# Residual kept in the experts' sum banks, and five or six more buffers for weights

## The chip, the cores and the metric

One core of a Trainium2 chip runs the whole program. The metric is the time of the program on the device in microseconds (us), the median of several executions. The core has a matrix engine (TensorE, PE in the profile), VectorE (DVE), ScalarE (ACT), GpSimd (POOL) and SyncE (SP), which here only issues the DMA transfers. On-chip memory is SBUF (128 partitions) and, for the sums of TensorE, PSUM with eight banks of 512 float32 a partition.

## The reference

A decoder of two layers over 256 tokens of width 1024, all in float32. Layer 0 has a Mamba-2 mixer, layer 1 a sliding-window attention mixer; both also attend to 256 memory tokens. Each layer ends in a mixture of 32 gated experts, of which each token uses two of one group. Cut to what matters:

```python
for layer in range(2):
    h = h + mixer(h)                      # ssd_memory_mixer / swa_memory_mixer
    xt = rms_norm(h)
    gates = route(xt)                     # top-1 group, top-2 experts in it
    out = 0
    for e in range(32):
        he = silu(xt @ w_gate[e]) * (xt @ w_up[e])       # 1024 -> 512
        out = out + gates[:, e:e + 1] * (he @ w_down[e]) # 512 -> 1024
    h = h + out
return rms_norm(h, final_norm_w)
```

One expert's three matrices are 6 MiB, all experts of both layers 384 MiB. Every one is read once.

## The kernel before

**Stages.** `mixer_a`, the experts of layer 0 (`moe(c, 0)`), `mixer_b`, the experts of layer 1, `final_norm`. Each is a block of five instruction streams, one per engine, with semaphores between them; a block starts when all engines have left the one before.

**Weight slots.** Every weight is loaded in pieces of 1 MiB (a "job", `GRAN` = 2048 float32 a partition) into a slot. There are 11 `own` slots, 6 in `late` (in the mixers `late` is working memory) and `extra`: 18. `place_jobs` hands the slots out in turn, oldest first; `free` is the list. SP issues the jobs strictly in order (`load_job`, L255), each after a wait until the job that had the slot before is used (`before`, `released`, in the mixers `tile_used` and `late_free`). In the mixer's block SP issues the mixer's own tiles and then the first `FIRST_JOBS` = 18 jobs of the experts, all that fits; the others are issued in the experts' block.

**Experts.** A layer's 32 experts are eight quads of four. The first four quads in the order of load are worked off as two "wide" units each, of two experts with up to 64 tokens each; the other four as one "narrow" unit each, of four experts with up to 32 tokens. So 12 units, eight of 12 jobs and four of 24. A quad's place is found on the chip: VectorE sorts the quads by their fullest expert (`order`, L1365 to L1381, 13 steps, then `over`), SP and VectorE read the result into registers (`quads`, seven loads). SP does so before job 24, since the jobs before it belong to quad 0, always first. A unit on TensorE: gate and up in two halves (`gate_up`, L1498), gather of the next unit's tokens (L1473, scaled by VectorE in `gathered`, L1343), transposes, down in two halves (`down`, L1507), gates' transposes, and `scatter` (L1490), four matmuls (eight records of the profile) that add to four banks `sums` = banks 0 to 3, started afresh in unit 0. In layer 0 units 9 and 10 are preceded by `side`: keys and values of the memory for layer 1, from `memT1`, into `mkT1` and `mv1`.

**Residual.** The residual h lies in SBUF (8 KiB a partition). The mixer adds its output to it (`Router.dve`, L533); the normalised rows for the experts are written to `xs`. After the experts, `finish_h` (L436) adds the four banks to h, at the head of `mixer_b` and of `final_norm`. After the router TensorE does four matmuls of the identity with constants, whose result nobody uses (`Router.pe`, L517, eight records).

**Overflow.** Experts with more tokens than a unit holds are done in `over_rounds` at the end of the block. It needs the register `most`, which each engine loads there. With these inputs the branch isn't taken.

**Working buffers.** `xbcT`, `xnT`, `qT`, `acc` and small ones of mixer A, `xnT`, `qtok`, `qmT` of mixer B, and the experts' `pick`, `gated`, `xg`, `silu`, `hid`, `turned`, `gates_T`, `y` and `rank` are allocated stage by stage beside the slots.

Of the kernel before, what the change touches and what calls it, by code (L numbers as in the profile page):

```python
# [28 lines left out]
P = 128  # L29
# [22 lines left out]
OWN, LATE = 11, 6  # L52
SLOTS = OWN + LATE + 1
# [54 lines left out]
def place_jobs():  # L108
# [14 lines left out]
    free = free[:-8] + LATE_A + free[-8:]  # L123
    for layer in range(2):
        for job in expert_jobs(layer):
            slot = free.pop(0)
            put(job, slot)
            free.append(slot)
        if layer == 0:
# [6 lines left out]
            free = LATE_B[:2] + own[:-6] + LATE_B[2:] + own[-6:]  # L136
# [10 lines left out]
OVER_SLOTS = [slot for slot in range(SLOTS) if slot not in KEPT]  # L147
# [25 lines left out]
class Core:  # L173


    def __init__(self, nc, ins, out, ctx):
        self.nc, self.ins, self.out, self.ctx = nc, ins, out, ctx
        self.small = self.sb("small", SMALL)
        self.h = self.sb("h", NT * D)
        self.xs = self.sb("xs", NT * D)  # L180
# [13 lines left out]
        self.own = self.sb("own", OWN * GRAN)  # L194
        self.late = self.sb("late", LATE * GRAN)
        self.extra = self.sb("extra", GRAN)
# [5 lines left out]

    def carve_late(self, *sizes):
        assert sum(sizes) <= LATE * GRAN
        return [self.late[:, sum(sizes[:i]):sum(sizes[:i + 1])] for i in range(len(sizes))]
# [22 lines left out]
    def slot(self, job):  # L228
        n = JOB_AT[job][0]
        if n == OWN + LATE:  # L230
            return self.extra[:, :]
        return self.own[:, n * GRAN:(n + 1) * GRAN] if n < OWN else self.late[:, (n - OWN) * GRAN:(n - OWN + 1) * GRAN]
# [66 lines left out]
class Units:  # L299
# [4 lines left out]
    def __init__(self, core, order, freed, holds=None, first=0):  # L304
# [7 lines left out]
        free, user, self.of, self.before = [*range(first, NBANK), *range(first)], {}, {}, {}  # L312
# [133 lines left out]
class Router:  # L446
# [4 lines left out]
    SEMS = "h_new n2_act n2_dve x2T_act x2T_dve rw_ready rt_dve rt_act counted"  # L451
# [46 lines left out]
    def pe(self, pe, key):  # L498
# [123 lines left out]
def mixer_a(c):  # L622
# [12 lines left out]
    with ctx:  # L635
        sb = lambda name, n: c.sb("a_" + name, n, ctx)
        xbcT = sb("xbcT", 12 * SEQ)
# [3 lines left out]
        xnT = sb("xnT", KD * SEQ)  # L641
        mem = memnT
        qT = sb("qT", 1024)
        mT = qT
        acc = sb("acc", 3 * SEQ)
# [3 lines left out]
        cbm2 = sb("cbm", 2 * P)  # L649
# [10 lines left out]
        dtb = [sb(f"dt{i}", 2 * SSD_HEADS) for i in range(6)]  # L660
        dtx, t_, s_, s2, dt, adt = dtb
        ea, eac, toend, acum = sb("ea", 24), sb("eac", 24), sb("toend", 24), sb("acum", 48)
        smc = sb("smc", 64)
        gss = sb("gss", 8)
# [64 lines left out]
        late_free = [U.at["yT", 7]] * 4 + [U.at["mk", 3], U.at["pv", 3], U.at["yo", 3]]  # L729
# [3 lines left out]
        def _(sp):  # L733
# [39 lines left out]
            for job in expert_jobs(0)[:FIRST_JOBS]:  # L773
# [3 lines left out]
                else:  # L777
# [417 lines left out]
class Experts:  # L1195
# [13 lines left out]
    def allocate(self, ctx):  # L1209
        c, layer = self.c, self.layer  # L1210
        sb = lambda name, n: c.sb(f"e{layer}_{name}", n, ctx)
        self.pick = sb("pick", NT * P)
        self.gated = sb("gated", NT * P)
        self.xg = sb("xg", KD * P)
        self.silu = sb("silu", DE)
        self.hid = sb("hid", DE)
        self.turned = sb("turned", DE)
        self.gates_T = sb("gates_T", SEQ)
        self.y = [sb(f"y{i}", 512) for i in range(2)]
        self.rank = sb("rank", 7 * QUADS * QUADS)  # L1220
        self.sums, (self.b_gate, self.b_up, self.b_gather, self.b_turn) = c.banks[0:4], c.banks[4:8]
# [855 lines left out]
```

## Time and profile before

| what | value |
|---|---|
| runs, median (lowest to highest) | 1386.57 us (1385.32 to 1391.3), 3 runs |
| profiled execution, its own time | 1383.7 us |
| its span, first to last instruction | 1381.9 us |
| mean granted TensorE clock | 0.956 |
| PE busy | 1227.8 us, 89% |
| DVE, ACT, POOL busy | 281.3, 203.9, 32.7 us |
| HBM read | 460.91 MB |
| mean over the span | 334 GB/s |

The page cuts the span into 40 slices of 34.5 us; one line gives the GB/s that the 16 DMA engines moved in each. PE's busy time counts overlapping matmuls once, and a busy PE is not PE at its peak. A timeline row gives the start, the duration, the engine and line, the operation, how many alike are merged (xN) and, in brackets, the engine's idle time before it with what ended it. Rows on SPq are issues of transfers; their duration is that of issuing, not of moving data.

### The profile page before, as it was taken

What the parts mean: (1) busy time and instruction counts of PE and PEld (TensorE: products, weight loads), DVE (VectorE), ACT (ScalarE), POOL (GpSimd) and SP (SyncE); (2) the same over time, 40 slices, a digit from 0 to 9 for tenths busy, and PEclk for the clock granted to TensorE, in tenths of its full rate; (3) what the DMA queues carried; (4) which work ended last, traced back from release to release, by engine and by line L of the source; (5) the groups of instructions that cost most, each with busy time, mean ns of one, the idle gap of its engine ahead of it and who ended that gap; (6) DMA issues with size and microseconds to landing.
All of it is one profiled execution on the core that took longest, in us unless ns stands there. A gap on an engine that the chain in (4) does not pass through costs nothing. (4 is left out here: it accounts for less than half of the span.)

```text
span 1381.9 us, 15072 instructions
## 1 busy us (share of the span) xinstructions
PE 1227.8 (89%) x6036; PEld 608.3 (44%) x6036; DVE 281.3 (20%) x683; ACT 203.9 (15%) x488; POOL 32.7 (2%) x42
## 2 busy tenths in 40 slices
PE   6999999999999998877778998999999999657685
PEld 5875764544444443432323566454444444222221
DVE  3842551221111111010102164031111111000101
ACT  2233231300000000000002255120000000000001
POOL 0001200000000000000000011000000000000000
PEclk9999999999999999989899999999999999887897
DMA  9731178479999999999999612559999999999994
GB/s 347 294 122 54 52 286 340 183 304 421 420 422 421 421 422 414 423 416 421 421 421 355 231 61 92 212 196 422 420 422 420 421 421 421 421 421 422 421 421 180
DMA packets 81241, 463.03 MB, mean 335 GB/s; under 512 B 7392, under 2 KB 9488, under 8 KB 32016
## 3 DMA queue, kind: packets, MB, share of 16 engines
q1 hardware_dynamic: 81168, 462.02, 82.3%
q8 instruction: 51, 0.84, 0.2%
q14 instruction: 22, 0.18, 0.0%
HBM read 460.91 MB, written 1.07 MB: 334 GB/s over the span
## 5 line engine op out<-in xcount | busy, mean ns | idle before, releaser
L1498 PE MATMUL bank<-own,e_xg 128*64 128x512 f32 (+1 forms) x1272 | 267.4, 635 | 36.2 <-DMA own<-in_w_gate 10.1
L1498 PE MATMUL bank<-late,e_xg 128*32 128x512 f32 (+1 forms) x648 | 162.9, 648 | 16.2 <-DMA own<-in_w_up 7.7
L1498 PEld LDWEIGHTS bank<-own,e_xg 128*64 128x64 f32 (+1 forms) x1272 | 78.3, 130 | 199.0 <-issue 198.9
L1507 PE MATMUL bank<-own,e_turned 128*64 128x512 f32 (+1 forms) x576 | 131.0, 685 | 32.0 <-DMA own<-in_w_down 19.7
L1390 DVE TENSOR_TENSOR e_hid<-e_silu,bank 128x512 f32<-128x512 f32 x24 | 25.6, 1067 | 502.6 <-ACT e_silu L1441 502.6
L1507 PE MATMUL bank<-late,e_turned 128*32 128x512 f32 (+1 forms) x408 | 94.9, 671 | 25.2 <-DMA own<-in_w_down 11.3
L1473 PEld LDWEIGHTS bank<-e_pick,xs 128*128 128x128 f32 x768 | 89.6, 192 | 19.6 <-issue 19.6
L1473 PE MATMUL bank<-e_pick,xs 128*128 128x128 f32 x768 | 95.5, 278 | 0.0
L1441 ACT ACTIVATE e_silu<-bank 128x512 f32<-128x512 f32 x24 | 14.3, 597 | 539.5 <-PE bank L1498 539.5
L1498 PEld LDWEIGHTS bank<-late,e_xg 128*32 128x32 f32 (+1 forms) x648 | 45.6, 131 | 96.7 <-issue 96.6
L1490 PE MATMUL bank<-e_y,e_gates_T 128*128 128x512 f32 x192 | 86.5, 593 | 1.4 <-ACT e_gates_T L1449 1.4
L1507 PEld LDWEIGHTS bank<-own,e_turned 128*64 128x64 f32 (+1 forms) x576 | 36.7, 137 | 103.0 <-issue 94.1
L401 PE MATMUL bank<-a_xnT,own 128*128 128x256 f32 x320 | 70.1, 380 | 0.0
L1395 DVE COPY e_y<-bank 128x512 f32<-128x512 f32 x24 | 16.6, 691 | 254.3 <-PE bank L1507 254.3
L401 PEld LDWEIGHTS bank<-a_xnT,own 128*128 128x128 f32 x320 | 60.4, 190 | 8.4 <-issue 0.4
L1498 PE MATMUL bank<-extra,e_xg 128*64 128x512 f32 (+1 forms) x128 | 59.7, 610 | 0.0
L1507 PEld LDWEIGHTS bank<-late,e_turned 128*32 128x32 f32 (+1 forms) x408 | 25.8, 134 | 73.1 <-issue 66.2
L1490 PEld LDWEIGHTS bank<-e_y,e_gates_T 128*128 128x128 f32 x192 | 34.6, 190 | 36.3 <-issue 34.4
L1447 ACT ACTIVATE e_y<-bank 128x512 f32<-128x512 f32 x24 | 14.3, 597 | 241.6 <-PE bank L1507 241.6
L1516 PE MATMUL bank<-small 128*128 128x512 f32 x88 | 41.9, 622 | 2.6 <-PEq L1624 1.3
L1343 DVE TENSOR_TENSOR e_xg<-bank,small 128x512 f32<-128x512 f32 x48 | 33.2, 692 | 48.2 <-PE bank L1473 48.2
L401 PE MATMUL bank<-own,a_xnT 128*128 128x512 f32 x96 | 42.1, 593 | 0.0
(357 smaller groups left out, 1124.1 us busy)
## 6 DMA issues: line engine op xcount, KB each, us to landing
own<-in_w_gate SPq DMA_DIRECT2D x81, 1024.0 KB, 13.1
own<-in_w_up SPq DMA_DIRECT2D x78, 1024.0 KB, 12.6
own<-in_w_down SPq DMA_DIRECT2D x72, 1024.0 KB, 13.4
late<-in_w_down SPq DMA_DIRECT2D x51, 1024.0 KB, 13.4
late<-in_w_gate SPq DMA_DIRECT2D x42, 1024.0 KB, 13.6
late<-in_w_up SPq DMA_DIRECT2D x39, 1024.0 KB, 12.5
own<-in_a_in_w SPq DMA_DIRECT2D x17, 1024.0 KB, 14.3
extra<-in_w_up SPq DMA_DIRECT2D x11, 1024.0 KB, 14.4
```

The costliest lines, as they stand in the source:

```text
L401: ins = pe.matmul(out, lhsT(k), rhs(k), start=(k == 0), stop=(k == n - 1))
L1343: dve.tensor_tensor(cut(self.xg[:, 512 * half:512 * half + 512], k=4), cut(bank, k=4), spread_last(c.f(f"ffn_norm{layer}", 4 * half, 4 * h ...
L1390: dve.tensor_tensor(self.hid[:, :].rearrange("q (h j p) -> q h p j", h=2, j=2), by_half(self.silu), by_half(self.b_up), ALU.mult).then_inc ...
L1395: dve.tensor_copy(self.y[1][:, :], self.b_down[1][:, :]).then_inc(s["y_ready"], 1)
L1441: act.activation(self.silu[:, :], self.b_gate[:, :], ACT.Silu).then_inc(s["silu_done"], 1)
L1447: act.activation(self.y[0][:, :], self.b_down[0][:, :], ACT.Copy).then_inc(s["y_ready"], 1)
L1473: ins = pe.matmul(bank[:, k * P:(k + 1) * P], xs[:, t, 4 * half + k, :], cut(self.pick, t=NT)[:, t, :], start=(t == 0), stop=(t == NT - 1))
L1490: ins = pe.matmul(self.sums[2 * t + out][:, :], self.gates_T[:, t * P:(t + 1) * P], self.y[out][:, :], start=first, stop=last, skip_group_ ...
L1498: ins = pe.matmul(bank[q * T:(q + 1) * T, :], self.xg[:, at:at + T], cut(tile(q), k=4)[:, k, :], start=(half == 0 and k == 0), stop=(half ...
L1507: ins = pe.matmul(self.b_down[out][q * T:(q + 1) * T, :], self.turned[:, at:at + T], cut(tile(q), j=2)[:, j, 512 * out:512 * out + 512], s ...
L1516: pe.matmul(self.b_turn[:, :], c.f("ident"), c.small[:, 0:512], start=True, stop=True)
```

## The change

1. `dynamic_dma_scratch_size=512` is given to the program (default before), and with the SBUF that this and the rest frees there are 12 own slots and up to six others: EXTRA as before, XNT (`xnT`), TAIL (the first 8 KiB of one common working buffer `work`), RES (`h`), MKV (`mkT1` and `mv1` together), MEMT (`memT1`). `place_jobs` puts MKV first and TAIL, XNT, RES last in layer 0 and leaves MKV out from unit 9 on; in layer 1 MEMT is first, MKV in the middle and TAIL, XNT, RES last. The mixers load the first 23 and 24 jobs.
2. After the router TensorE multiplies the identity with h into the four sum banks, in place of the four matmuls with constants. The experts' scatter adds to that. The stages after copy the banks (two by VectorE, two by ScalarE) or read them directly in the last norm. The banks are 0, 3, 4, 7 in layer 0 and 0, 5, 6, 7 in layer 1.
3. `order` goes ahead of the two `gathered` of the first unit, since its scratch now shares a buffer with `silu`; `y` shares `silu` and `hid`.
4. The load of `most` goes from the end of the block to the place after `quads` (SP, DVE) and after unit 0 (ACT, PE). The table for the square root is loaded in the last unit. The vector of the final norm is loaded after the last weights instead of at the start of the block.

```diff
-OWN, LATE = 11, 6
-SLOTS = OWN + LATE + 1
+OWN, LATE = 12, 6
+SLOTS = OWN + LATE + 6
+EXTRA, XNT, TAIL, RES, MKV, MEMT = range(OWN + LATE, SLOTS)
+SUMS = [[0, 3, 4, 7], [0, 5, 6, 7]]
+WORK = GRAN + 3328
...
-    free = free[:-8] + LATE_A + free[-8:]
+    free = [MKV] + free[:-8] + LATE_A + free[-8:] + [TAIL, XNT, RES]
     for layer in range(2):
         for job in expert_jobs(layer):
             slot = free.pop(0)
+            if slot == MKV and layer == 0 and (job[0] == "mem" or job[2] >= SIDE[0]):
+                slot = free.pop(0)
             put(job, slot)
             free.append(slot)
...
-            free = LATE_B[:2] + own[:-6] + LATE_B[2:] + own[-6:]
+            free = [MEMT] + LATE_B[:2] + own[:-6] + [LATE_B[2], MKV] + LATE_B[3:] + own[-6:] + [TAIL, XNT, RES]
...
-FIRST_JOBS = SLOTS
+FIRST_JOBS = [SLOTS - 1, SLOTS]
...
-def finish_h(c, dve, q, signal):
-
-    hq = c.h[:, 512 * q:512 * q + 512]
-    dve.tensor_tensor(hq, hq, c.banks[q][:, :], ALU.add).then_inc(signal, 1)
+def copy_h(c, layer, q):
+
+
+    return c.h[:, 512 * q:512 * q + 512], c.banks[SUMS[layer][q]][:, :]
...
-            for _ in range(4):
-                pe.matmul(out[:, :], c.f("ident"), c.small[:, 0:512], start=True, stop=True)
+            pe.wait_ge(s["h_new"], 4)
+            for q in range(4):
+                ins = pe.matmul(c.banks[SUMS[self.layer][q]][:, :], c.f("ident"), c.h[:, 512 * q:512 * q + 512], start=True, stop=True)
+            ins.then_inc(s["h_kept"], 1)
...
-        late_free = [U.at["yT", 7]] * 4 + [U.at["mk", 3], U.at["pv", 3], U.at["yo", 3]]
+        late_free = [U.at["yT", 7]] * 4 + [U.at["mk", 3], U.at["pv", 3], U.at["yo", 3], U.at["router", 1], U.at["out", 3]]
...
-            for job in expert_jobs(0)[:FIRST_JOBS]:
+            for job in expert_jobs(0)[:FIRST_JOBS[0]]:
                 prev, slot = before(job), JOB_AT[job][0]
                 if prev:
                     sp.wait_ge(*tile_used(prev[1]))
-                else:
+                elif slot == RES:
+                    sp.wait_ge(s["h_kept"], 1)
+                    sp.wait_ge(s["n2_act"], 6)
+                elif slot != MKV:
                     sp.wait_ge(c.units_done, late_free[slot - OWN] + 1)
...
+        self.y, self.rank = [self.silu, self.hid], self.silu
+        self.sums = [c.banks[i] for i in SUMS[layer]]
...
-                if layer == 1:
-                    final_w = c.ins["final_norm_w"].rearrange("(o n) -> o n", o=1)
-                    sp.dma_start(c.memT1[:, 0:D], final_w.broadcast_to([P, D])).then_inc(c.final_w, 16)
                 for n, job in enumerate(jobs):
-                    if n < FIRST_JOBS:
+                    if n < FIRST_JOBS[layer]:
                         continue
                     if job == ("expert", layer, 2, "gate", 0, 0):
-                        quad = self.quads(sp)
+                        quad, most = self.quads(sp), self.beyond(sp)
...
                 pick(0)
+                order()
                 for half in range(2):
                     dve.wait_ge(s["gathered"], half + 1)
                     gathered(half, s["xg_ready"], (self.b_gather, self.b_turn)[half])
-                order()
-                quad = self.quads(dve)
+                quad, most = self.quads(dve), self.beyond(dve)
...
-                    ins = scatter(u == 0, last)
+                    ins = scatter()
...
                 for u in range(NU):
                     unit(u)
+                    if u == 0:
+                        most = self.beyond(pe)
...
+            for q in (2, 3):
+                act.activation(*copy_h(c, 0, q), ACT.Copy).then_inc(s["h_act"], 1)
...
-            for q in (0, 2, 1, 3):
-                finish_h(c, dve, q, s["h_whole"])
+            for q in (0, 1):
+                dve.tensor_copy(*copy_h(c, 0, q)).then_inc(s["h_dve"], 1)
...
+                for half in range(2):
+                    act.activation(waste[:, 2 * t + half, :], copy_h(c, 1, 2 * t + half)[1], ACT.Square, scale=1.0 / 32,
+                                   accum_out=ss[:, 2 * t + half:2 * t + half + 1]).then_inc(s["act"], 1)
...
-                hv = cut(c.h, t=NT)[:, t, :]
-                dve.scalar_tensor_tensor(out=hv, in0=hv, scalar=r[t], in1=w, op0=ALU.mult, op1=ALU.mult).then_inc(s["done"], 1)
+                for half in range(2):
+                    to, bank = copy_h(c, 1, 2 * t + half)
+                    dve.scalar_tensor_tensor(out=to, in0=bank, scalar=r[t], in1=w[:, 512 * half:512 * half + 512], op0=ALU.mult,
+                                             op1=ALU.mult).then_inc(s["done"], 1)
...
-    nc = bacc.Bacc("TRN2", target_bir_lowering=False, num_devices=1)
+    nc = bacc.Bacc("TRN2", target_bir_lowering=False, num_devices=1, dynamic_dma_scratch_size=512)
```

## Rows read from the trace of the kernel before

**Rows 1.** GB/s moved in each of the page's 40 slices.

```profile
GB/s 347 294 122 54 52 286 340 183 304 421 420 422 421 421 422 414 423 416 421 421 421 355 231 61 92 212 196 422 420 422 420 421 421 421 421 421 422 421 421 180
```

**Rows 2.** Busy time by stretch, a narrow unit; last columns clock, DMA, GB/s.

```profile
1260.00:1280.00 20.00, 12.74 (x64) 3.16 (x64) 0.00 (x0) 0.00 (x0) 0.00 (x0) 0.66 1.01 421
```

**Rows 3.** Timeline of ScalarE, SiLU of units 1 and 8.

```profile
324.42 0.60 ACT L1441 ACTIVATE e_silu<-bank 128x512 f32<-128x512 f32 x1 [18.60 <-PE bank L1498]
...
530.88 0.60 ACT L1441 ACTIVATE e_silu<-bank 128x512 f32<-128x512 f32 x1 [18.61 <-PE bank L1498]
```

**Rows 4.** Waits of TensorE, 285 to 525 us: sum, times, longest.

```profile
PE bank L1507 <- ACT e_turned L1444: 3.8, 8, 0.5
```

**Rows 5.** Waits of TensorE, 525 to 760 us, the longest.

```profile
PE bank L1507 <- DMA own<-in_w_down: 16.8, 5, 5.8
```

**Rows 6.** Waits of TensorE, 745 to 913 us, the longest of nine.

```profile
PE bank L356 <- ACT late L1781: 3.4, 3, 1.4
```

**Rows 7.** Busy time by stretch, at the first release of layer 0.

```profile
282.00:284.00 2.00, 2.00 (x13) 0.59 (x10) 1.69 (x10) 0.00 (x0) 0.00 (x0) 1.00 0.00 0
...
286.00:288.00 2.00, 2.00 (x12) 0.72 (x10) 0.00 (x0) 0.00 (x0) 0.00 (x0) 1.00 0.85 328
```

**Rows 8.** Timeline of SP's queue, layer 0: transfers issued.

```profile
265.80 1.06 SPq L255 DMA_DIRECT2D own<-in_w_gate  x2
284.62 0.80 SPq L255 DMA_DIRECT2D own<-in_w_up  x2
...
291.49 0.81 SPq L255 DMA_DIRECT2D late<-in_w_down  x2
296.61 0.90 SPq L255 DMA_DIRECT2D late<-in_w_gate  x2
...
314.11 0.81 SPq L255 DMA_DIRECT2D own<-in_w_up  x2
```

**Rows 9.** Timeline around the start of the experts of layer 1.

```profile
903.72 0.80 SPq L255 DMA_DIRECT2D own<-in_w_gate  x2
...
906.89 3.68 PE L517 MATMUL bank<-small 128*128 128x512 f32 x8
...
924.03 0.33 SPq L255 DMA_DIRECT2D late<-in_w_up  x1
```

**Rows 10.** Timeline of the routing and first unit, layer 0.

```profile
268.96 3.68 PE L517 MATMUL bank<-small 128*128 128x512 f32 x8
...
275.47 0.43 DVE L1332 TENSOR_TENSOR e_pick<-small,pos 128x256 f32<-128x256 f32 x1 [0.33 <-PEq L635]
...
279.25 0.69 DVE L1343 TENSOR_TENSOR e_xg<-bank,small 128x512 f32<-128x512 f32 x1 [3.35 <-PE bank L1473]
...
281.64 0.18 DVE L1365 TENSOR_REDUCE e_rank<-counts 128x8 f32<-128x32 f32 x1
...
284.59 0.29 DVE L1381 SCALAR_TENSOR_TENSOR over<-pos,e_rank 128x32 f32<-128x32 f32 x2
...
289.19 0.43 DVE L1338 TENSOR_TENSOR e_gated<-e_pick,gates 128x256 f32<-128x256 f32 x1 [4.31 <-issue]
```

**Rows 11.** Timeline from the last scatter of layer 0 into the mixer.

```profile
739.14 3.67 PE L1490 MATMUL bank<-e_y,e_gates_T 128*128 128x512 f32 x8 [0.70 <-ACT e_gates_T L1449]
...
744.04 2.48 DVE L436 TENSOR_TENSOR h<-h,bank 128x512 f32<-128x512 f32 x4 [5.22 <-PEq L1287]
...
745.38 3.40 PE L340 MATMUL bank<-small,h 128*128 128x128 f32 x16 [2.57 <-DVE h L436]
```

**Rows 12.** Timeline of the last norm.

```profile
1372.45 2.48 DVE L436 TENSOR_TENSOR h<-h,bank 128x512 f32<-128x512 f32 x4 [5.59 <-PEq L1287]
...
1373.82 1.04 ACT L1977 ACTIVATE xs<-h 128x1024 f32<-128x1024 f32 x1
...
1377.50 1.28 DVE L1993 SCALAR_TENSOR_TENSOR h<-h,norm_r,memT 128x1024 f32<-128x1024 f32 x1
```

**Rows 13.** DMA queues: kind, packets, MB, share of 16 engines.

```profile
q1 hardware_dynamic: 81168, 462.02, 82.3%
```

More of the change, by code:

```diff
@@ L201, in sb, with carve, carve_work @@
         return (ctx or self.ctx).enter_context(self.nc.sbuf_tensor(name, [P, n], F32))
+    def carve(self, whole, *sizes):
+        return [whole[:, sum(sizes[:i]):sum(sizes[:i + 1])] for i in range(len(sizes))]
     def carve_late(self, *sizes):
         assert sum(sizes) <= LATE * GRAN
-        return [self.late[:, sum(sizes[:i]):sum(sizes[:i + 1])] for i in range(len(sizes))]
+        return self.carve(self.late, *sizes)
+    def carve_work(self, *sizes):
+        assert sum(sizes) <= WORK
+        return self.carve(self.work, *sizes)
     def sem(self, name):
@@ L229, in slot @@
         n = JOB_AT[job][0]
-        if n == OWN + LATE:
-            return self.extra[:, :]
+        if n >= OWN + LATE:
+            return {EXTRA: self.extra, XNT: self.xnT, TAIL: self.work[:, 0:GRAN], RES: self.h, MKV: self.mkv1, MEMT: self.memT1}[n][:, :]
         return self.own[:, n * GRAN:(n + 1) * GRAN] if n < OWN else self.late[:, (n - OWN) * GRAN:(n - OWN + 1) * GRAN]
@@ L299, with __init__ @@
 class Units:
-    def __init__(self, core, order, freed, holds=None, first=0):
+    def __init__(self, core, order, freed, holds=None, first=()):
         self.core, self.freed = core, freed
@@ L311, in __init__ @@
         held = [key for keys in holds.values() for key in keys]
-        free, user, self.of, self.before = [*range(first, NBANK), *range(first)], {}, {}, {}
+        free, user, self.of, self.before = [*first, *[b for b in range(NBANK) if b not in first]], {}, {}, {}
         for key in order:
@@ L659, in mixer_a @@
         yT = xbcT[:, 0:12 * SEQ]
[L660 to L664, printed above, removed]
+        dtx, t_, s_, s2, ea = c.carve(c.memT1, 48, 48, 48, 48, 24)
+        eac = c.over[:, 0:24]
         def channels(j):
@@ L1207, in __init__, with allocate @@
         self.side = SIDE if layer == 0 else []
-    def allocate(self, ctx):
+    def allocate(self):
         c, layer = self.c, self.layer
[L1211 to L1221, printed above, removed]
+        _, self.pick, self.gated, self.xg, self.silu, self.hid, self.turned, self.gates_T = c.carve_work(
+            GRAN, NT * P, NT * P, KD * P, DE, DE, DE, SEQ)
+        self.y, self.rank = [self.silu, self.hid], self.silu
+        self.sums = [c.banks[i] for i in SUMS[layer]]
+        self.b_gate, self.b_up, self.b_gather, self.b_turn = (c.banks[i] for i in range(NBANK) if i not in SUMS[layer])
         self.b_down = [self.b_gate, self.b_up]
@@ L1485, in turn_gates, with scatter @@
                     ins.then_inc(signal, 1)
-                def scatter(first, last):
+                def scatter():
                     for t in range(NT):
@@ L1667, in freed @@
                     "out": (s["h_new"], i + 1)}[kind]
-        U = Units(c, order, freed, holds, first=4)
+        U = Units(c, order, freed, holds, first=[b for b in range(NBANK) if b not in SUMS[0]])
         R = Router(c, U, s, 1, xnT, qmT[:, 0:512])
@@ L1696, in _ @@
                     c.load_mixer_half(sp, n, half)
-            for job in expert_jobs(1)[:FIRST_JOBS]:
+            for job in expert_jobs(1)[:FIRST_JOBS[1]]:
                 prev, slot = before(job), JOB_AT[job][0]
@@ L1700, in _ @@
                     sp.wait_ge(*tile_used(prev[1]))
-                elif late_free[slot - OWN] is not None:
+                elif slot == RES:
+                    sp.wait_ge(s["h_kept"], 1)
+                    sp.wait_ge(s["n2_act"], 6)
+                elif slot == MKV:
+                    sp.wait_ge(c.units_done, U.at["pv", 3] + 1)
+                elif slot != MEMT and late_free[slot - OWN] is not None:
                     sp.wait_ge(c.units_done, late_free[slot - OWN] + 1)
@@ L1956, in final_norm @@
 def final_norm(c):
-    s = c.sems("final", "h_whole act dve done")
+    s = c.sems("final", "act dve done")
     stored = [c.sem(f"stored{t}") for t in range(NT)]
-    w = c.memT1[:, 0:D]
-    ss, r = ([v[:, t:t + 1] for t in range(NT)] for v in (c.norm_ss, c.norm_r))
+    w, waste = c.memT1[:, 0:D], cut(c.work[:, 0:4 * 512], q=4)
+    ss, r = c.norm_ss, ([c.norm_r[:, t:t + 1] for t in range(NT)])
     with c.nc.Block() as block:
```

99 lines of the change are left out of this document (48 added, 51 removed).

## The prediction

> **What bounds the kernel now.** I read the GB/s line of the page first [rows 1]. It has two flat stretches: from the tenth slice to the twenty-first and from the twenty-eighth to the thirty-ninth, the two expert stages, it stands at 414 to 423. In the two mixers it falls to 52 and 61. So the whole kernel moves its bytes at one rate, and loses time where it moves none. The expert weights are 192 transfers of 1 MiB in each layer, plus four for the memory keys in the first; at 421 GB/s one takes 1.0486/0.421 = 2.49 us.
>
> Next, whether that stream or TensorE sets the end of an expert stage. The SiLU of unit 1 stands at 324.42 and that of unit 8 at 530.88 [rows 3]: 206.46/7 = 29.49 us for a unit of 12 transfers, which need 12 x 2.49 = 29.9 us. In these eight "wide" units TensorE never waits for a transfer; its only wait is 3.8 us on a copy [rows 4]. So TensorE is barely faster than the stream there and eats its reserve by 0.4 us a unit. The four narrow units have 24 transfers (59.8 us) for about the same TensorE work. There it waits for weights (16.8 us for one kind alone) [rows 5] and is busy 12.74 of 20 us with the stream at 421 [rows 2]. The end of both expert stages is therefore the last weight's landing: the moment from which the stream ran without a gap, plus what was still to load. In the second mixer, between the stages, its longest sum of waits is 3.4 us, on a copy, and none is on a DMA [rows 6]. So filling more slots before the unbroken stream begins takes 2.49 us a slot off the end, as long as the slots are filled in time that is idle today.
>
> The idle time: in the first layer the stream stands still at 282 to 284 and is at 328 GB/s in 286 to 288, after the first release at 284.62 [rows 7, 8]. That is a lag of about 1.5 us from issue to data, so data flow without a break from 286.1. In the second the last prefill is issued at 903.72 (four MB at most behind it), and the next load only at 924.03 [rows 9], data from 925.5.
>
> **The change, part by part.** *More slots.* The first layer starts with 23 filled instead of 18, the second with 24 instead of 18. The DMAs are the same in number and bytes; they only move ahead. The two kinds:
> - MKV, the twelfth own slot, and in the second layer MEMT are free long before; the GB/s line shows the room (183 in the eighth slice, 196 in the twenty-seventh) [rows 1].
> - TAIL, XNT and RES come free only in the routing. First layer: TAIL with the last own pair, at 265.8 [rows 8]; XNT when the router's matmuls end, before 268.96; RES when the four identity matmuls have read h. They stand where the four warming matmuls stand today, 268.96 to 272.64 (eight records) [rows 10], so about 272.7; SP's queue holds only this load until then. Data: from 267.3, four transfers until 277.3, RES until 279.8. Margin to 286.1: 6 us. Second layer: two own and TAIL at 903.72, data 905.2 to 912.7; XNT to 915.2; RES, free at 906.89 + 3.68 = 910.6 [rows 9], to 917.7. Margin to 925.5: 8 us.
>
> Gain 5 x 2.49 = 12.5 us and 6 x 2.49 = 14.9 us.
>
> *What SP must do at a worse moment.* Before job 24 SP reads the order of the quads, now eight register loads instead of seven. Before, that was the seventh load of the stage and hidden behind the backlog: SP finished an issue at 291.49 + 0.81 = 292.30, the next came at 296.61 [rows 8]; VectorE has the same 4.31 us gap, for the same seven loads, ahead of its instruction at 289.19 [rows 10]. So 0.62 us each, 4.9 us for eight. In the first layer job 23 still waits for the first release; then come the loads, then job 24. Issues at 284.62 and 284.62 + 0.4 + 4.9 = 289.9; data of job 23 run 286.1 to 288.6, those of job 24 begin at 291.4. The stream is idle 2.8 us: cost 2.8 us (bounds: nothing, if the loads overlap the wait, and 4.9 us). Behind SP only the loads are queued; after 291.4 eleven jobs can be queued by 305 (until 318.8), the next is issued at 314.11 [rows 8], so no second gap. In the second layer 24 slots are filled, so the loads come before the first wait. Order ends 5.5 us before the first release (279.1 and 284.62, worked out below), the loads take 4.9. Cost nothing.
>
> *The order of quads moves ahead of the scaling of the gathered rows.* It takes 284.59 + 0.29 - 281.64 = 3.2 us. The pick ends at 275.90, so order runs to 279.1; the first half of the gather lets VectorE go at 279.25 [rows 10]. Hidden with 0.1 us to spare: taken as nothing, at most 0.5 us a layer; 3.2 us a layer if that gather were not there to cover it.
>
> *Residual in the sum banks.* The identity matmuls are 512 columns wide like those which they replace; the mask that follows is the later event or equal. Nothing; bound 1 us a layer, if TensorE starts them late. The scatters accumulate in any case: unchanged. The shared buffers (y in those of silu and hid) add no wait, since TensorE does the scatter before the next unit's gate and up, which come before the next silu.
>
> *Stage ends.* The scatter ends at 739.14 + 3.67 = 742.8, the next stage's first instruction is at 744.04: 1.2 us, of which 0.62 is the register load of the overflow count, now done after unit 0. Then four adds take 2.48 us on VectorE, and TensorE starts before the fourth, at 745.38 [rows 11]. Now two copies on VectorE beside two on ScalarE: TensorE starts after one of each, 0.69 us like VectorE's other 512-column reads of a bank [rows 10]. Saved: 0.62 + (745.38 - 744.04 - 0.69) = 1.3 us; bounds 0.6 and 2. The load on TensorE's queue after unit 0, 0.6 us, falls in the wide units, where TensorE has slack to the stage's end.
>
> *Last norm.* From 1372.45 to 1378.78 [rows 12] it is 6.3 us: two adds (1.3), square (1.04 + 0.1), scale, root and reciprocal (0.8), product 1.28, then the second half's scalars and product. After: squares of two banks (2 x 0.7 from ScalarE's 0.60 for 512 columns [rows 3] and its accumulator read), scalars 0.7, two products of 0.69, scalars 0.6, two products: 1.4 + 0.7 + 1.4 + 0.6 + 1.4 = 5.5. Saved 0.8, and 0.6 for the register load: 1.4 us; bounds 0 and 2.5. The final gain vector (0.5 MB, 1.25 us of the stream) is loaded behind the last weights, in place of the stage's start; TensorE works on those weights for 3.6 us and scatters for 3.7 before the vector is wanted. Nothing.
>
> *Sum.* 12.5 - 2.8 + 14.9 + 1.3 + 1.4 = 27.3 us. The profiled execution took 1383.7 us, 2.9 us under the median 1386.6 (0.2%), so it gives 1356.4, and beside the median **1359.3 us**, 2.0% faster.
>
> **Two rules weighed.** The stream runs at about 421 GB/s in the flat slices [rows 1]. The Trainium skill, "DMA: Bandwidth & Descriptors", section Specifications, gives about 358 GB/s as the HBM limit of a core; by it a slot would be worth 2.93 us and the eleven slots 32.2 us instead of 27.4, an estimate from that page; the trace disagrees with it and decides. The second speaks to the scratch: the queue of kind hardware_dynamic moved 462.02 of the 463.03 MB, and no queue of a software kind is listed [rows 13]. The Trainium skill's "SBUF — State Buffer", section on the size of SBUF, says that the scratch is the ring for software-generated descriptors; by it the shrunken scratch costs nothing here.
>
> **Rivals.**
> 1. *The forecast*, 70%: 1353 to 1366 (from the bounds: gap at SP 0 to 4.9, stage ends and norm up to 2 less or 2 more, clock of the last units, some 2 us).
> 2. *The wide units become the bound.* If a unit rises over 29.9 us, the stream starves and gives the lead back. At 30.9 us, seven units in two layers: 14 us lost, 1373. For it: the margin is only 0.4 us. Against: no instruction is added within a unit. 7%.
> 3. *The three late slots come too late*, since SP waits for them in order: only two and three slots count, 5 x 2.49 + 2.7 - 2.8 = 12.4 us, about 1374. Against: margins of 6 and 8 us. 7%. A further 7% for smaller losses together, 1364 to 1376.
> 4. *No change*: the lead is gained, but the stream breaks later and ends with today's last transfer. The next release comes just when the backlog of the first refill ends (286.1 + 12 x 2.49 = 316.0; the issue at 314.11 [rows 8] gives data from 315.6). But the backlog grows by 0.4 us a unit. About 1384, with the stage ends alone; 5%.
> 5. *Slower: fewer transfers in flight.* Should the hardware queue use the scratch, transfers would come one after another, each with the lag of 1.5 us: 352 transfers, +528 us, some 1890. It decides from 0.08 us a transfer (27.3/352). Against it: the queue kinds [rows 13]. 4%.
>
> **How the numbers follow.** Likeliest 1359.3. The range 1352 to 1373 takes in case 1 with the bounds and most of 2 and the smaller losses; left out are parts of 2, 3, 4 and 5, about 18%. Case 1's own range is 1353 to 1366. Half a per cent is 7 us, about what a measurement can tell. Faster 0.91 (cases 1 to 3), same 0.05, slower 0.04.
>
> **What would show it.** DMA idle before the first release should shrink to about 5 us in the first expert stage, followed by one load, a dip of some 3 us, and then 421; the second starts with no dip. The unit period stays 29.5 us. The first narrow waits for weights come later, the second mixer starts 9 to 10 us earlier and the last sum about 26 us earlier. Wrong, if the unit period is over 29.9, if the stream has holes in the wide units, if RES's load is issued after the first release, or if the rate itself falls below 415.

## The result and the profile after

The changed kernel takes 1351.76 us (median of 4 runs, 1350.94 to 1353.17) against 1385.94 us for the one before: ratio 0.9746, 95% interval 0.9726 to 0.9766, 34.2 us or 2.5% less. The forecast was 1359.3 with 1352 to 1373. The direction and most of the mechanism were right; the time is 7.5 us below the forecast and 0.2 us below the range. Measured once more later, the same kernel took 1353.79 us, inside the range, so that edge alone says little. What the forecast lacked is a mechanism, shown below. The profiled execution took 1350.94 us (span 1349.2) against 1383.7: 32.8 us less, where the sum had 27.3.

The bytes moved in each of the page's slices, in GB/s, after; it answers to [rows 1].

```profile
GB/s 359 328 125 25 47 252 424 188 307 427 427 427 426 427 427 424 427 424 427 427 427 367 319 63 125 187 219 417 426 426 424 425 425 426 426 427 427 426 427 180
```

From the tenth slice to the twenty-first and from the twenty-ninth to the thirty-ninth the stream moves 424 to 427 GB/s, not 414 to 423. No part of the change was costed as touching that rate. At 427, one transfer of 1 MiB takes 1.0486/0.427 = 2.456 us instead of 2.49.

SP's queue in layer 0, in the timeline of the kernel after (start us, duration, place, operation, tiles); it answers to [rows 8].

```profile
266.72 0.43 SPq L270 DMA_DIRECT2D work<-in_w_down  x1
269.24 0.33 SPq L270 DMA_DIRECT2D xnT<-in_w_down  x1
272.75 0.33 SPq L270 DMA_DIRECT2D h<-in_w_down  x1
284.70 0.33 SPq L270 DMA_DIRECT2D mkv<-in_w_down  x1
289.94 0.90 SPq L270 DMA_DIRECT2D own<-in_w_gate  x2
```

The same stretch by windows, after (the columns of [rows 2]; the last is GB/s); it answers to [rows 7].

```profile
280.00:284.00 4.00, 4.00 (x24) 1.95 (x24) 0.71 (x2) 0.00 (x0) 0.00 (x0) 1.00 0.02 4
286.00:288.00 2.00, 2.00 (x12) 0.65 (x10) 0.85 (x2) 0.00 (x0) 0.00 (x0) 1.00 0.77 303
288.00:290.00 2.00, 2.00 (x12) 0.65 (x10) 0.00 (x0) 0.00 (x0) 0.00 (x0) 1.00 0.44 184
290.00:292.00 2.00, 2.00 (x12) 0.72 (x10) 0.00 (x0) 0.00 (x0) 0.00 (x0) 1.00 0.44 86
292.00:294.00 2.00, 2.00 (x12) 0.64 (x10) 0.00 (x0) 0.00 (x0) 0.00 (x0) 1.00 0.98 406
```

This part reads like the forecast. TAIL (work), XNT and RES (h) are issued at 266.72, 269.24 and 272.75, against 265.8, "before 268.96" and about 272.7 predicted. The stream is empty before the first release at 284.70, one load follows, then a dip, and the next issue is at 289.94 (predicted 289.9).

SiLU of units 1 and 8 in ScalarE's timeline, after; it answers to [rows 3].

```profile
324.50 0.60 ACT L1453 ACTIVATE work<-bank 128x512 f32<-128x512 f32 x1 [18.60 <-PE bank L1514]
...
530.96 0.60 ACT L1453 ACTIVATE work<-bank 128x512 f32<-128x512 f32 x1 [18.61 <-PE bank L1514]
```

206.46/7 = 29.49 us a unit, to the hundredth what it was. The wide units did not become slower; but at 427 GB/s their twelve transfers now need 12 x 2.456 = 29.47 us, so the stream and TensorE are level there.

From the last unit of layer 0 into the second mixer, timeline of the kernel after; it answers to [rows 11].

```profile
704.98 1.28 ACT L1459 ACT_TABLE_LOAD   x1
...
723.73 3.67 PE L1506 MATMUL bank<-work 128*128 128x512 f32 x8 [0.70 <-ACT work L1463]
...
727.94 1.28 ACT L1736 ACT_TABLE_LOAD   x1 [4.35 <-PEq L1298]
727.97 1.29 DVE L1913 COPY h<-bank 128x512 f32<-128x512 f32 x2 [4.55 <-PEq L1298]
729.23 1.09 ACT L1736 ACTIVATE h<-bank 128x512 f32<-128x512 f32 x2
...
729.97 1.94 PE L355 MATMUL bank<-small,h 128*128 128x128 f32 x16 [2.57 <-ACT h L1736]
...
735.76 1.28 ACT L1758 ACT_TABLE_LOAD   x1
```

The scatter starts at 723.73 against 739.14: 15.4 us earlier, where the forecast said 9 to 10. VectorE's first instruction of the next block stands 727.97 - 727.40 = 0.57 us after its end, against 744.04 - 742.81 = 1.23 before. These 0.66 us fit the 0.62 of the register load that was moved out of the way; no run moves it alone. But TensorE starts 729.97 - 727.97 = 2.00 us after that instruction, against 745.38 - 744.04 = 1.34 in [rows 11]: ScalarE's first copy waits for a table load of 1.28 us (it puts another set of ScalarE's function tables in place), and TensorE waits for that copy. The two cancel.

The end, timeline of the kernel after; it answers to [rows 12] and, for the scatter, stands against 1367.19 before.

```profile
1334.03 3.67 PE L1506 MATMUL bank<-work 128*128 128x512 f32 x8 [0.70 <-ACT work L1463]
...
1338.38 1.28 ACT L1997 ACT_TABLE_LOAD   x1 [4.49 <-ACTq L1298]
1339.67 0.60 ACT L1997 ACTIVATE work<-bank 128x512 f32<-128x512 f32 x1
...
1340.96 1.28 ACT L2000 ACT_TABLE_LOAD   x1
...
1344.68 1.41 DVE L2014 SCALAR_TENSOR_TENSOR h<-bank,norm_r,memT 128x512 f32<-128x512 f32 x2
```

The last scatter starts 33.2 us earlier (forecast: about 26). From its start to the end of the last product it is 12.06 us, where it was 1377.50 + 1.28 - 1367.19 = 11.59: the last norm lost 0.5 us instead of saving 1.4. Its first function waits for one table load and its root for a second. Before, one load stood at the head of that block, beside the first two of VectorE's adds of [rows 12], which took about as long:

```profile
1372.41 1.28 ACT L1974 ACT_TABLE_LOAD   x1 [5.37 <-PEq L1287]
```

So the span's 1381.9 - 1349.2 = 32.7 us are 33.2 at the scatter less 0.5 behind it.

### The profile page after: what moved, and what is told of

Read it like the earlier page. It is cut to its first block and busy times, and to the rows that moved or that the text cites. A ratio compares the mean times of both kernels' runs of the same rounds, so it can differ in the third digit from the quotient of the medians.

```text
span 1349.2 us, 15082 instructions
## 1 busy us (share of the span) xinstructions
PE 1218.0 (90%) x6036; PEld 607.2 (45%) x6036; DVE 277.8 (21%) x679; ACT 210.3 (16%) x498; POOL 32.7 (2%) x42
## 5 line engine op out<-in xcount | busy, mean ns | idle before, releaser
L1514 PE MATMUL bank<-own,work 128*64 128x512 f32 (+1 forms) x1176 | 282.5, 617 | 26.8 <-DMA own<-in_w_up 10.0
L1514 PEld LDWEIGHTS bank<-own,work 128*64 128x64 f32 (+1 forms) x1176 | 81.2, 128 | 166.0 <-issue 166.0
L1514 PE MATMUL bank<-late,work 128*32 128x512 f32 (+1 forms) x536 | 142.8, 634 | 12.9 <-DMA own<-in_w_up 12.9
L1523 PE MATMUL bank<-own,work 128*32 128x512 f32 (+1 forms) x416 | 111.3, 647 | 24.4 <-DMA h<-in_w_down 12.3
L1489 PEld LDWEIGHTS bank<-work,xs 128*128 128x128 f32 x768 | 90.3, 193 | 19.8 <-issue 19.8
L1489 PE MATMUL bank<-work,xs 128*128 128x128 f32 x768 | 96.2, 279 | 0.0
L1506 PE MATMUL bank<-work 128*128 128x512 f32 x192 | 86.5, 593 | 1.4 <-ACT work L1463 1.4
L1523 PE MATMUL bank<-late,work 128*64 128x512 f32 (+1 forms) x256 | 76.1, 709 | 11.1 <-DMA own<-in_w_down 5.5
L416 PE MATMUL bank<-xnT,own 128*128 128x256 f32 x384 | 84.7, 380 | 0.0
L416 PEld LDWEIGHTS bank<-xnT,own 128*128 128x128 f32 x384 | 72.3, 190 | 10.0 <-issue 0.4
## 6 DMA issues: line engine op xcount, KB each, us to landing
h<-in_w_down SPq DMA_DIRECT2D x12, 1024.0 KB, 13.8
```

Source lines behind the costliest of these rows:

```text
L416: ins = pe.matmul(out, lhsT(k), rhs(k), start=(k == 0), stop=(k == n - 1))
L1489: ins = pe.matmul(bank[:, k * P:(k + 1) * P], xs[:, t, 4 * half + k, :], cut(self.pick, t=NT)[:, t, :], start=(t == 0), stop=(t == NT - 1))
L1506: ins = pe.matmul(self.sums[2 * t + out][:, :], self.gates_T[:, t * P:(t + 1) * P], self.y[out][:, :], start=False, stop=True, skip_group_ ...
L1514: ins = pe.matmul(bank[q * T:(q + 1) * T, :], self.xg[:, at:at + T], cut(tile(q), k=4)[:, k, :], start=(half == 0 and k == 0), stop=(half ...
L1523: ins = pe.matmul(self.b_down[out][q * T:(q + 1) * T, :], self.turned[:, at:at + T], cut(tile(q), j=2)[:, j, 512 * out:512 * out + 512], s ...
```

## The experiments

Two questions were open: what raised the rate, and what each part is worth without it. Two facts of the change bear on the first. The buffers are allocated in another order, and the full diff has one line that the shortened diff above does not show, a buffer that nothing reads or writes (`edge`, in `Core.__init__`):

```diff
+        self.sb("edge", 96)
+        self.own = self.sb("own", OWN * GRAN)
+        self.late = self.sb("late", LATE * GRAN)
```

96 floats are 384 bytes in each partition. Worked out from the sizes of what is allocated ahead, and taking that buffers are padded to 32 bytes and that the program keeps 128 bytes below the first, the slots (own) begin at byte 1024 of each partition after, a multiple of 256; before they began at 42624, 128 bytes past one. No trace shows an address; only the differences between the runs below (384, 256, 64 bytes and so on) are exact. Each 1 MiB transfer writes one row of 8 KiB in each of 128 partitions, so all rows share that offset. My theory was that this is the rate's cause; the rival was the smaller scratch of the transfers. The totals blur small differences, so a second measure is read from every run's trace: the time from the first release of layer 0 (the mkv load; before, the own load at 284.62) to the start of the last scatter of that layer. For layer 1 it is the same from the first load issued in the experts' block (memT; before, the late load at 924.03). Neither stretch holds the first mixer, whose length differs by several microseconds between executions of the same code (the RES load is issued at 272.75 in one execution of the changed kernel and at 275.23 in another).

**Without the unused buffer** (the changed kernel, slots from byte 640).

```diff
-        self.sb("edge", 96)
```

> The changed kernel without the 384 unused bytes ahead of the slots: every slot then starts at 128 bytes past a multiple of 256, as in the kernel before, instead of on a multiple of 1024. Nothing else differs. Theory A, the start address of the slots sets the rate of the stream: back to 421 GB/s in the expert stages from 427, 8 KB packets spread over 300 to 320 ns instead of 300 to 305, and some 870 us of streaming take 1.4% longer, so 12 us more, about 1364 us. Rival B, the smaller scratch or another part of the change raised the rate: stays at 427 GB/s and 1352 us.

Measured: 1362.09 us (1359.62 to 1366.65), ratio to before 0.9812 (0.9775 to 0.9848). The bytes by slice:

```profile
GB/s 346 335 124 24 47 252 411 189 309 422 421 422 420 421 421 414 422 416 420 422 421 360 350 62 124 185 220 420 420 422 421 421 421 422 421 422 421 421 421 181
```

Back to 420 to 422 with two slices at 414 and 416, as before the change, with everything else in place. Packet by packet it is the same: from 320 to 520 us the 8 KiB packets took 309.5 ns in the mean in the changed kernel, 314.0 in the kernel before and 313.9 here, 1.5% more. The rate is worth 1362.09 - 1351.76 = 10.3 us by the medians (9.1 by the ratios, 0.9812 and 0.9746, whose intervals do not overlap), and the change without it 1387.75 (the kernel before beside this run) - 1362.09 = 25.7, or 26.1 by the ratio, against the 27.3 of the sum.

**The kernel before with the unused buffer** ahead of its slots (from byte 43008, a multiple of 256), nothing else changed.

```diff
+        self.sb("edge", 96)
         self.own = self.sb("own", OWN * GRAN)
```

> The kernel before with 384 unused bytes ahead of the slots, so that each of the 18 slots starts on a multiple of 1024. Nothing else differs. Theory A: 427 GB/s, 12 to 13 us off 1386, about 1373.5 us, still 18 slots. Rival B: 421 GB/s and 1386 us. If the rate rises but the time falls by less than 8 us, TensorE and not the stream sets more of the end than I held.

Measured: 1373.97 us (1371.61 to 1376.43), ratio 0.9899 (0.9867 to 0.993): 13.8 us less by the medians. By slice:

```profile
GB/s 359 287 123 55 47 265 372 184 265 426 418 424 426 427 426 423 427 424 426 427 427 365 251 62 93 187 207 425 425 422 426 427 427 426 427 426 427 426 426 187
```

One unused buffer gives the kernel before 424 to 427 in most flat slices (418, 422 and 423 in three) and one per cent, with the scratch at its default and `small`, `h` and `xs` where they were. From first release to last scatter of layer 0 it is 734.33 - 285.29 = 449.0 us, 5.5 less than before (454.5), much as in the changed kernel (6.2, 445.2 against 439.0); in layer 1 it is 437.9 against 443.2. That the totals differ by 13.8 here and 10.3 there is within the ranges of the runs.

**The kernel before with the smaller scratch.**

```diff
-    nc = bacc.Bacc("TRN2", target_bir_lowering=False, num_devices=1)
+    nc = bacc.Bacc("TRN2", target_bir_lowering=False, num_devices=1, dynamic_dma_scratch_size=512)
```

> The kernel before with the scratch cut to 512 bytes and nothing else: all addresses move down by 15872 bytes, so the slots keep their 128 bytes past a multiple of 256. Theory A: 421 GB/s and 1386 us, no change. Rival B (the scratch itself costs rate): 427 GB/s, about 1373.5 us. The rival of the prediction, fewer transfers in flight: clearly slower than 1386.

Measured: 1386.48 us (1383.23 to 1390.36), ratio 0.9995 (0.9977 to 1.0013), flat slices at 415 to 422, as before, and 454.9 us from first release to last scatter of layer 0 against 454.5. The scratch neither costs nor gives; it moves the slots to byte 26752, again 128 past a multiple of 256, and the rate stays. The rival for the rate falls, and so does the forecast's rival 5.

**Three more start addresses** of the changed kernel: 256 bytes short of 1024 (768), 192 past a multiple (704), 64 past (832). The diff is the first; the second has 16 and the third 48 in place of 32.

```diff
-        self.sb("edge", 96)
+        self.sb("edge", 32)
```

> The changed kernel with 128 instead of 384 unused bytes: the slots start on a multiple of 256, but 256 past a multiple of 512. If 256 bytes is the step that counts: 427 GB/s and 1352 us. If 512 or 1024 is: 421 GB/s and 1362 us.

> The changed kernel with 64 unused bytes: the slots start 192 past a multiple of 256 (and on a multiple of 64). If what costs is each packet's touching one more block of 256 bytes, whatever the part: as at 128 past, 421 GB/s and 1362 us. If the cost goes with the bytes between the block's start and the packet's (192 of 8192 bytes, 2.3%, against 1.6% at 128): about 418 GB/s and 1370 us. If a multiple of 64 is enough: 427 GB/s and 1352 us.

> The changed kernel with 192 unused bytes: the slots start 64 past a multiple of 256. One more block per packet, whatever the part: 421 GB/s and 1362 us. Cost by the bytes ahead of the packet (64 of 8192, 0.8%): 424 GB/s and 1358 us. A multiple of 64 is enough: 427 GB/s and 1352 us.

Measured, with the commonest value of the flat slices of each page and the time from first release to last scatter of each layer:

| slots begin at byte | past a multiple of 256 | median us (range) | ratio to before (95%) | flat slices GB/s | layer 0 us | layer 1 us |
|---|---|---|---|---|---|---|
| 1024 (changed kernel) | 0 | 1351.76 (1350.94-1353.17) | 0.9746 (0.9726-0.9766) | 427 | 439.0 | 424.3 |
| 1024 (the same, again) | 0 | 1353.79 (1351.23-1355.3) | 0.976 (0.9738-0.9783) | 427 | 439.1 | 423.6 |
| 768 | 0 | 1353.62 (1350.57-1354.35) | 0.9771 (0.9755-0.9787) | 427 | 440.1 | 423.7 |
| 832 | 64 | 1363.59 (1357.54-1363.71) | 0.9829 (0.9809-0.985) | 421 | 445.5 | 427.9 |
| 640 | 128 | 1362.09 (1359.62-1366.65) | 0.9812 (0.9775-0.9848) | 421 | 445.2 | 428.7 |
| 704 | 192 | 1363.55 (1361.21-1365.34) | 0.9829 (0.9805-0.9853) | 421 | 445.1 | 427.9 |

Two groups and nothing between them in the last three columns; of single totals one, 1357.54, lies between. A multiple of 256 is enough (768 is none of 512); a multiple of 64 or 128 is not; how far off the start is makes no difference that these runs can tell. Layer 0 differs by 6 us, and its 196 - 23 = 173 transfers times 2.491 - 2.456 = 0.035 are 6.1. Layer 1 differs by 4.3 us. Together that is 10.2 us, where the totals give 10.3 by the medians above and 8.9 by the mean ratios of the two groups (0.9823 and 0.9759).

The Trainium skill, "DMA: Bandwidth & Descriptors", section How a descriptor splits into AXI transactions, says that a transaction must start on a multiple of 256 bytes, so that a descriptor that starts elsewhere begins with a transaction from the boundary below, whose bytes ahead of the start are fetched and cost beats. The section speaks of reads, and the change moves the address that is written. An estimate by that page's beats of 32 bytes, with a row of 8 KiB as one descriptor, gives 258, 260 and 262 for 256 at 64, 128 and 192 past (0.8, 1.6 and 2.3% more). The runs show about 1.4% at each, so the cost did not go with those bytes; it may be a price for one transaction more in each row (33 for 32), which no run here separates. How it is made up was not measured.

**Without the three late slots** (TAIL, XNT, RES in neither layer; the changed kernel otherwise).

```diff
-    free = [MKV] + free[:-8] + LATE_A + free[-8:] + [TAIL, XNT, RES]
+    free = [MKV] + free[:-8] + LATE_A + free[-8:]
-            free = [MEMT] + LATE_B[:2] + own[:-6] + [LATE_B[2], MKV] + LATE_B[3:] + own[-6:] + [TAIL, XNT, RES]
+            free = [MEMT] + LATE_B[:2] + own[:-6] + [LATE_B[2], MKV] + LATE_B[3:] + own[-6:]
-FIRST_JOBS = [SLOTS - 1, SLOTS]
+FIRST_JOBS = [SLOTS - 4, SLOTS - 3]
```

> The changed kernel without TAIL, XNT and RES as slots: 20 and 21 instead of 23 and 24, all else as it is. The slots' theory: six transfers fewer ahead, 6 x 2.455 = 14.7 us later, less the 2.8 us hole at the start of the first expert stage, which goes, since the register loads then come behind a backlog: 1363.7 us, stream at 427 GB/s. Rival: the late slots bring nothing since TensorE's wide units (29.5 us) leave no room for them: 1352 us.

Measured: 1363.97 us (1363.11 to 1365.6), ratio 0.9822 (0.9795 to 0.9849): 12.2 us above the changed kernel's median, 11.9 expected. With 20 slots filled the register loads come later, behind a backlog; the stretch from first release to last scatter of layer 0 is 730.47 - 286.78 = 443.7 us, 4.7 more than 439.0, and three slots less the hole are 3 x 2.456 - 2.8 = 4.6. From the last scatter of layer 0 to that of layer 1 it is 616.6 against 610.3, 6.3 more where three slots are 7.4. So the late slots do come in time, each is worth about one transfer, and the forecast's rivals 3 and 4 fall.

**The register loads before the first wait** (the changed kernel, SP's eight loads moved to the head of the block).

```diff
+                quad, most = self.quads(sp), self.beyond(sp)
                 for n, job in enumerate(jobs):
                     if n < FIRST_JOBS[layer]:
                         continue
-                    if job == ("expert", layer, 2, "gate", 0, 0):
-                        quad, most = self.quads(sp), self.beyond(sp)
```

> The changed kernel with one edit: SP makes its eight register loads at the head of the experts' block, before its first wait for a slot, instead of between job 23 and job 24. They need the order of the quads, which is there at 278.8 in the changed kernel, and take 4.9 us, so they end about 283.8, before the first release at 284.6. Theory: the hole in the stream goes, and with it the 2.8 us that the prediction charged: 2 GB/s windows without a dip after 286, 0.2% faster than the changed kernel, about 1349. Rival: the hole costs nothing, since the stream catches up in the wide units: 1352.

Measured: 1349.46 us (1348.32 to 1353.77), ratio 0.975 (0.9732 to 0.9768). SP's queue and the windows of this run (same columns as above):

```profile
286.79 0.33 SPq L270 DMA_DIRECT2D mkv<-in_w_down  x1
287.33 3.39 SPq L270 DMA_DIRECT2D own<-in_w_gate  x2
```

```profile
290.00:292.00 2.00, 2.00 (x12) 0.72 (x10) 0.00 (x0) 0.00 (x0) 0.00 (x0) 1.00 1.01 426
```

The next load follows the first release by 0.54 us instead of 5.24, and the stretch that held the dip runs at 426. From first release to last scatter it is 724.39 - 286.79 = 437.6 us: 1.4 us less than 439.0, of the 2.8 expected. In the total it cannot be told from the changed kernel, whose interval overlaps. The hole is real and where it was said to be. At its place it costs what was said, too: GB/s in the 20 us after the first release, in this run and in the changed kernel (same columns).

```profile
286.79:306.79 20.00, 19.53 (x100) 7.65 (x96) 2.61 (x4) 1.25 (x3) 0.00 (x0) 1.00 0.95 390
284.70:304.70 20.00, 19.53 (x100) 7.65 (x96) 2.61 (x4) 1.26 (x3) 0.00 (x0) 1.00 0.83 329
```

(390 - 329) x 20 us is 1.2 MB, or 2.9 us of the stream. By the bytes of the packets this lead is 0.9 MB (2.1 us) after 200 us and 0.7 MB (1.6 us) after 400. The first flat slices of this run stand at 423, 426, 421 and 425, where the changed kernel has 427, 427, 427 and 426. So the lead is gained and partly lost again on the way; at the stage's end 1.4 us of it is left here and 1.6 and 2.1 in the two kernels with the same edit below (437.4 and 436.9). What lowers the rate there is not shown.

**The table loads.** The root's table is asked for by a small root at the head of both blocks, and VectorE alone copies the four banks in the second mixer. The last line of the diff stands at the head of ScalarE's part of the last norm.

```diff
         def _(act):
-            for q in (2, 3):
-                act.activation(*copy_h(c, 0, q), ACT.Copy).then_inc(s["h_act"], 1)
+            act.activation(c.norm_r[:, 6:7], c.norm_ss[:, 4:5], ACT.Sqrt)
...
-            for q in (0, 1):
+            for q in (0, 2, 1, 3):
...
+            act.activation(c.norm_r[:, 6:7], c.norm_ss[:, 4:5], ACT.Sqrt)
```

> The changed kernel with its two stage entries altered: VectorE alone copies the four banks to h in the second mixer, in the order 0, 2, 1, 3, and ScalarE runs one root at the head of the mixer and of the last norm, as in the kernel before. The root in the last unit stays. Theory C, the table loads on ScalarE ate the gain of the stage ends: in the mixer TensorE starts 1.4 us after the block instead of 2.0, in the last norm one table load of 1.28 us less lies on the chain: 1.7 us less together, up to 2.4, about 1350. Rival: both table loads were hidden and nothing moves, 1352.

Measured: 1349.19 us (1347.5 to 1351.2), ratio 0.9741 (0.9725 to 0.9756). Its timeline, the two block heads:

```profile
730.94 1.28 ACT L1735 ACT_TABLE_LOAD   x1 [4.35 <-PEq L1298]
730.97 2.48 DVE L1910 COPY h<-bank 128x512 f32<-128x512 f32 x4 [4.56 <-PEq L1298]
...
732.31 2.28 PE L355 MATMUL bank<-small,h 128*128 128x128 f32 x16 [1.91 <-DVE h L1910]
```

```profile
1333.23 3.67 PE L1506 MATMUL bank<-work 128*128 128x512 f32 x8 [0.71 <-ACT work L1463]
...
1337.42 1.28 ACT L1992 ACT_TABLE_LOAD   x1 [4.33 <-PEq L1298]
...
1338.83 0.58 ACT L1995 ACTIVATE work<-bank 128x512 f32<-128x512 f32 x1
...
1342.88 1.41 DVE L2012 SCALAR_TENSOR_TENSOR h<-bank,norm_r,memT 128x512 f32<-128x512 f32 x2
```

TensorE starts 732.31 - 730.97 = 1.34 us after VectorE's first instruction instead of 2.00, and from the last scatter's start to the start of the last two products (the last row, x2) it is 9.65 us instead of 10.65. One table load stands at the head of each block and none between. Together 1.7 us, as expected. In the total this cannot be told from the changed kernel (0.9741 against 0.9746, the intervals overlap).

**Both edits together**, and the changed kernel once more beside them.

> Both edits together on the changed kernel: if both theories hold they add, 4.5 us, about 1347.3 us, 0.3% faster than the changed kernel. If only the register loads matter 1349, if only the tables 1350.

> The changed kernel itself, unaltered, beside the next one on the same chip. It should give 1351.8 us again, 0.9746 of the kernel before, within 0.2%. It is there because the two small edits moved the time by 2 us, which is as much as single runs of one kernel differ.

> The kernel with the register loads first and the stage entries without the table loads, once more, beside the changed kernel. If the two edits add as expected: 4.5 us below it, about 1347.3 us. If only what the traces show of the table loads (1.7 us) is real: 1350 us. If neither counts: the same time.

Measured: 1349.97 us (1349.13 to 1352.77), ratio 0.9745 (0.973 to 0.9759); then, side by side, the changed kernel 1353.79 (1351.23 to 1355.3), ratio 0.976 (0.9738 to 0.9783), and both edits 1351.53 (1345.42 to 1354.73), ratio 0.9734 (0.9707 to 0.976). The medians lie 1.8 and 2.3 us lower, the intervals overlap. The local savings repeat (9.65 and 9.64 us against 10.65 and 10.66 from the last scatter to the last product; 437.4 and 436.9 against 439.0 and 439.1 in layer 0), but I expected 4.5 us and that did not come. A version faster than the changed kernel is likely, by 0.1 to 0.2%, and not proven by the totals.

## Why the prediction was right, and where it was not

*What sets the end*: right. The last landing ends each expert stage, as both tests of it bear out. Leaving out three slots cost what the sum gives them, and a higher rate went straight into the total.

*The slots, 12.5 and 14.9 us*: right. With the slots at 421 GB/s (the run without the unused buffer) layer 0 from first release to last scatter took 445.2 us against 739.14 - 284.62 = 454.5: 9.3 us less, where the slots and the hole give 12.5 - 2.8 = 9.7. Layer 1 in the same run took 428.7 us against 1367.19 - 924.03 = 443.2: 14.5 less, where the slots give 14.9. The whole change at the old rate gave about 26 of 27.3 us (24.5 by the mean ratio of the three runs at that rate).

*The margins of the late slots*: right to 0.9 us in layer 0. In layer 1 TAIL, XNT and RES are issued at 889.86, 892.37 and 895.88, with the first release at 909.69.

*The hole at SP, 2.8 us*: right in place, in the time of the next issue (289.94 for 289.9) and in what it costs there (2.9 us); too large as a price at the stage's end, where removing it gave 1.4 to 2.1 us. The sum took every microsecond of lead as kept to the end.

*The unit period*: right. It stayed at 29.49 us, so rival 2 falls (it needed more than 29.9); at the higher rate its margin of 0.4 us shrank to 0.02 only because the stream became faster.

*The order of quads, the residual in the banks, the scratch*: nothing, as far as the runs tell. The scratch was tried alone; the other two were not. In the trace the gathered half still lets VectorE go at 279.33, and order ends before it at 279.14.

*The stage ends, 1.3 and 1.4 us*: wrong, 0 and -0.5 by the traces. The mixer's block began 0.66 us sooner after the scatter. All of it was given back: I costed ScalarE's first copy and the first squares at their own duration, with no term for a table load, and took the root's table, loaded in the last unit, as lasting into the next block. The trace loads a table again at the head of each, at 727.94 and 1338.38, though one was loaded at 704.98 in the last unit of layer 0, and then a second one for the root. Removing that from both blocks gave 1.7 us back. The Trainium skill's "ScalarE activation tables: per-element evaluation and per-set limits", section Table sets in the compiler and the runtime, says that the table loads are placed for each block. The trace agrees: 704.98 in one block, 727.94 in the next.

*The rate*: the step that failed. The prediction took 421 GB/s for both kernels ("the whole kernel moves its bytes at one rate") and its list of what could prove it wrong had only a lower rate. The change set the slots on a multiple of 256 bytes, and the rate rose to 427. A slot's worth of 2.49 us and the end of both streams rested on that rate. The rise is worth 9 to 10 us in the total, 6 of them in layer 0 and 4 in layer 1 by the stretches between release and scatter. The new address was to be seen in the diff, in a line of no evident use and in the new order of allocation, and neither my shortened diff nor my sum held them.

The sum over the whole, with what the runs show: 27.3, less 3.2 for the stage ends, plus about 1 for the hole, plus 9 to 10 for the rate, is 34 to 35 us; 34.2 were measured by the medians. That the forecast missed by no more than 7.5 us is in part luck: what it left out at the rate and what it promised too much at the stage ends have opposite signs.

In layer 1 the wide units move 424 to 426 GB/s where those of layer 0 move 426 and 427. Layer 1 starts without a hole, and layer 0 of the run with the register loads first, which has none either, shows the same kind of dip (421 to 426). That the two go together is seen; why is open.

## What to carry to other kernels

Where a stream of transfers sets the end, count what is in flight at the moment from which it never breaks again: here each slot filled ahead was worth about one transfer, and a late slot counted, since it landed before the stream could start again. Work out the start address of every buffer that such a stream writes, before and after an edit: here an unused buffer of 128 or 384 bytes was worth 9 to 14 us, more than three slots, and any edit of the allocation can lose it unseen. An estimate of a block's first function on ScalarE needs its table load (1.28 us here), whatever was loaded in the block before.

## What the runs showed of the hardware

- 1 MiB loads with rows of 8 KiB ran at up to 427 GB/s when the rows began on a multiple of 256 bytes in SBUF (by the worked-out addresses), and at 421 when they began 64, 128 or 192 bytes past one; a packet took 309.5 ns in the one and 314 in the other. I had not expected the written address to count, nor the price to be the same at each offset.
- The one core in use took 424 to 427 GB/s from HBM for over 400 us (twelve slices of 33.7 us).
- SP's eight register loads held its queue from the issue at 284.70 to the next at 289.94; moved ahead of the first wait, the next issue followed after 0.54 us.
- A table loaded on ScalarE at 704.98, at the end of one block, did not save a load of 1.28 us at 727.94, at the head of the next.
- The first mixer, the same code in all versions from the changed kernel on, took up to 6 us longer in one execution than in another (RES issued at 272.75 in the changed kernel and at 278.73 in the second run of both edits), more than the last edits were worth; a stretch between two marks in the trace told them apart where the total could not.
